# Compact RMS roots and paired projections in a two-layer diffusion backbone

## What is computed

```python
def _rmsnorm(x, w):
    xf = x.astype(jnp.float32)
    y = xf * lax.rsqrt(jnp.mean(xf * xf, axis=-1, keepdims=True) + NORM_EPS)
    return (y * w.astype(jnp.float32)).astype(x.dtype)
...
        h = _modulate(_rmsnorm(x, norm1_w[i]), sh1, sc1)
...
        o = o * lax.rsqrt(jnp.mean(o * o, axis=-1, keepdims=True) + NORM_EPS)
        return (jax.nn.silu(g) * o).reshape(b, l, hv).astype(dtype) @ w_out
...
    return _rmsnorm(x, final_norm_w)
```

## Time and profile before

| | |
|---|---|
| device time, median of 3 | 2215.78 us (2214.82 to 2217.1) |
| span of the profiled execution | 2214.5 us |
| that execution's own time | not given beside the span |
| TensorE matmul / weight load busy | 2022.2 us (91%) / 1728.0 us (78%) |
| VectorE busy | 1377.0 us (62%) |
| ScalarE busy | 764.3 us (35%) |
| GpSimd busy | 95.5 us (4%) |
| mean granted TensorE clock | 0.965 |
| chain that ended last | PE 75%, DVE 11%, issue 7%, ACT 4%, DMA 3% |

### The profile page before, as it was taken

One profiled execution on the slowest core, in us unless ns is written; L12 is line 12 of the kernel. 1 busy time (PEld: TensorE's weight loads), 2 busy tenths in 40 slices (PEclk: granted clock), 3 DMA queues, 4 the chain that ended last, 5 costly groups with the idle time before them and its releaser, 6 DMA issues.

```text
span 2214.5 us, 30605 instructions
## 1 busy us (share of the span) xinstructions
PE 2022.2 (91%) x10688; PEld 1728.0 (78%) x10688; DVE 1377.0 (62%) x2236; ACT 764.3 (35%) x1277; POOL 95.5 (4%) x161
## 2 busy tenths in 40 slices
PE   5899999999999869999999997889989779999996
PEld 5778878888887758888888886777777658788784
DVE  5665565564663677766664657667667467557376
ACT  3424223223323334312221333455545334323232
POOL 0000000000000000000000001210101000000000
PEclk9999999999999989999999998999999789999998
DMA  6230230230230112233224213211110122222222
GB/s 263 77 105 29 99 102 24 92 105 20 96 105 29 48 48 98 91 123 124 95 95 161 76 66 130 82 43 53 34 43 33 59 74 95 94 95 95 85 95 85
DMA packets 50748, 186.38 MB, mean 84 GB/s; under 512 B 5552, under 2 KB 5552, under 8 KB 50544
## 3 DMA queue, kind: packets, MB, share of 16 engines
q1 hardware_dynamic: 37248, 136.73, 17.9%
q0 software_dynamic: 13424, 48.63, 6.6%
HBM read 181.15 MB, written 4.19 MB: 84 GB/s over the span
## 4 chain that ended last, share of the span: by engine, by line
PE 75%; DVE 11%; issue 7%; ACT 4%; DMA 3%; DVEq 0%; SPq 0%; ACTq 0%; POOLq 0%
PE acc L370 60%; PE o_ps L452 4%; PE acc L561 4%; PE o_ps L540 3%; DMA ada_raw<-in_ada_dram 2%; PE acc L441 2%; PE acc L530 1%; DVE pt_lo L1369 1%; DVE h_lo L1099 1%; DMA x<-in_x_in_dram 1%; DVE ss L1027 1%; DVE nk_lo L1379 1%; DVE scratch L1090 1%; DVE w_lo L995 1%; ACT w_hi L669 1%
## 5 line engine op out<-in xcount | busy, mean ns | idle before, releaser
L370 PE MATMUL acc<-h_hi,w_hi 128*128 128x512 f32 (+1 forms) x1824 | 521.5, 351 | 41.5 <-DVE h_lo L1099 35.6
L370 PE MATMUL acc<-h_lo,w_hi 128*128 128x512 f32 (+1 forms) x1824 | 515.9, 348 | 0.0
L370 PE MATMUL acc<-h_hi,w_lo 128*128 128x512 f32 (+1 forms) x1824 | 515.6, 348 | 0.0
L669 ACT ACTIVATE w_hi<-raw 128x1024 fp32r<-128x1024 f32 x232 | 244.9, 1056 | 598.7 <-PE acc L370 598.5
L995 DVE TENSOR_TENSOR w_lo<-raw,w_hi 128x1024 fp32r<-128x1024 f32 x232 | 283.7, 1223 | 253.9 <-ACT w_hi L669 248.0
L370 PEld LDWEIGHTS acc<-h_hi,w_hi 128*128 128x128 f32 x1824 | 292.8, 189 | 96.4 <-issue 37.2
L370 PEld LDWEIGHTS acc<-h_hi,w_lo 128*128 128x128 f32 x1824 | 292.8, 189 | 45.5
L370 PEld LDWEIGHTS acc<-h_lo,w_hi 128*128 128x128 f32 x1824 | 292.9, 189 | 44.9
L370 PE MATMUL acc<-act_hi,w_hi 128*128 128x512 f32 (+1 forms) x528 | 163.0, 363 | 14.5 <-DVE act_lo L1273 12.2
L1113 DVE SCALAR_TENSOR_TENSOR x<-acc,mod,x 128x512 f32 (+3 forms) x136 | 81.9, 637 | 143.6 <-PE acc L370 138.6
L370 PE MATMUL acc<-act_lo,w_hi 128*128 128x512 f32 (+1 forms) x528 | 162.3, 361 | 0.0
(11 more groups left out here) (182 smaller groups left out, 2987.2 us busy)
## 6 DMA issues: line engine op xcount, KB each, us to landing
raw<-in_weights_dram SPq DMA_DIRECT2D x232, 512.0 KB, 3.3
ada_raw<-in_ada_dram POOLq DMA_DIRECT2D x80, 512.0 KB, 3.6
ada_start<-in_ada_first_dram SPq DMA_DIRECT2D x4, 2048.0 KB, 21.8
x<-in_x_in_dram SPq DMA_DIRECT2D x1, 3072.0 KB, 23.3
park_dram<-x POOLq DMA_DIRECT2D x1, 2048.0 KB, 8.1
rel<-in_bias_dram POOLq DMA_DIRECT2D x16, 128.0 KB, 2.4
x<-park_dram POOLq DMA_DIRECT2D x1, 2048.0 KB, 8.9
out_dram<-x SPq DMA_DIRECT2D x8, 256.0 KB, 2.0
```

The source lines that it names most:

```text
L370: mm = nc.tensor.matmul(tile[:, c0:c0 + cn], wt[:, b * P:(b + 1) * P], mv[:, n, c0:c0 + cn], start=(n == 0 and m == 0), stop=(n == last an ...
L669: nc.scalar.activation(w_hi[i][:, :], raw[i][:, :], ACT.Copy).then_inc(hi_split, 1)
```

## The change

`ss` is turned into token sums the other way round: each 128 x 128 piece of `ss` is the stationary operand and two columns of ones the moving one, so that the sums of 128 tokens come out one per partition; six such matmuls leave 128 x 6 sums (`token_sums`). ScalarE takes the root of 128 x 6 (after a root of one column that is issued before the wait), VectorE inverts 128 x 6 and multiplies the identity by it, which fills `ss` with six diagonal blocks. A matmul of ones by these blocks (`spread_roots`) leaves the inverse roots, the same in every partition, in the first two banks of `o_ps`; VectorE reads them from there. The sums lie in the fourth bank.

The two projections behind each norm become `project_two`: both weight chunks and both PSUM tiles are taken at once, and for each k all matmuls of both projections are issued, so that both end together. In layer 1 the values and keys then use the two tiles `acc[1]` and `acc[0]`. In the heads, the token sums follow gate chunk 1, the spread stands inside the projection of gate chunk 2 before its fourth k, the root and the inverse come before gate 1's Silu and its split. At the end one operation takes the place of two per chunk. (Left out below: declarations, `open_at` moved up, `take_keys` with the tile as an argument, the same edit of tallies.)

```diff
@@ -213,6 +214,8 @@
         o_ps = ctx.enter_context(nc.psum_tensor("o_ps", [P, VC, LAT], F32))
+        sums = o_ps[:, 3, 0:2 * TT]
+        spread = o_ps[:, 0:2, :].rearrange("p a t -> p (a t)")
         side = [o_ps[:, 2 * i:2 * i + 2, :].rearrange("p a t -> p (a t)") for i in range(2)]
...
@@ -382,7 +392,7 @@
                         pe.wait_ge(set_up, 1)
-                        ones_tile(KC, PARTS)
+                        token_sums(KC, TOK)
                     pe.wait_ge(ada_start_in[i], 16)
...
@@ -390,27 +400,54 @@
                 mm.then_inc(ada_started, 1)
-            def ones_tile(n, parts, on_side=False):
+                spread_roots(PARTS)
+            def token_sums(n, width):
                 pe.wait_ge(sq_added, squares_added.up(n))
-                tile = open_side(B.next_at(0)) if on_side else open_acc()
+                for t in range(width // P):
+                    mm = nc.tensor.matmul(sums[:, 2 * t:2 * t + 2], ss[:, t * P:(t + 1) * P], ones[:, 0:2], start=True, stop=True)
+                mm.then_inc(sums_done, 1)
+            def spread_roots(parts):
+                pe.wait_ge(diag_done, diags.up())
                 for c0, cn, _ in parts:
-                    mm = nc.tensor.matmul(tile[:, c0:c0 + cn], ones[:, :], ss[:, c0:c0 + cn], start=True, stop=True)
-                mm.then_inc(side_full if on_side else acc_full, 1)
+                    mm = nc.tensor.matmul(spread[:, c0:c0 + cn], ones[:, :], ss[:, c0:c0 + cn], start=True, stop=True)
+                mm.then_inc(spread_done, 1)
+            def project_two(parts, ready, tiles=None):
+                jobs = []
+                for j in range(2):
+                    w = next_chunk()
+                    jobs.append((open_acc() if tiles is None else open_at(tiles[j]), w))
+                for n in range(KC):
+                    ready(n)
+                    for tile, w in jobs:
+                        for m, (wt, mv) in enumerate(((w[0], h_hi), (w[0], h_lo), (w[1], h_hi))):
+                            for c0, cn, _ in parts:
+                                mm = nc.tensor.matmul(tile[:, c0:c0 + cn], wt[:, n * P:(n + 1) * P], mv[:, n, c0:c0 + cn],
+                                                      start=(n == 0 and m == 0), stop=(n == KC - 1 and m == 2))
+                        if n == KC - 1:
+                            mm.then_inc(acc_full, 1)
             def h_ready(first):
...
             def head_front(hd, first):
-                ready = None
                 if first:
                     ready = h_ready(h_split.now())
                     h_split.up(KC)
-                project(h_hi, h_lo, PARTS, ready)
-                value_tiles[0] = opened[0]
-                project(h_hi, h_lo, PARTS)
-                value_tiles[1] = opened[0]
+                    project_two(PARTS, ready)
+                    for n, i in enumerate((A.turn, 1 - A.turn)):
+                        value_tiles[n] = (i, A.taken[i].now())
+                else:
+                    project(h_hi, h_lo, PARTS)
+                    value_tiles[0] = opened[0]
+                    project(h_hi, h_lo, PARTS)
+                    value_tiles[1] = opened[0]
                 if not first:
...
@@ -474,8 +511,8 @@
                 project(h_hi, h_lo, PARTS)
-                ones_tile(VC, PARTS, on_side=True)
-                project(h_hi, h_lo, PARTS)
+                token_sums(VC, TOK)
+                project(h_hi, h_lo, PARTS, lambda n: spread_roots(PARTS) if n == 3 else None)
                 project(h_hi, h_lo, PARTS)
...
@@ -498,8 +535,9 @@
                     if first:
                         h_split.up(KC)
-                    with turns(pe, size, A.steps(2) + [(chunk, 2)]):
-                        project(h_hi, h_lo, parts, ready if first else None)
+                        project_two(parts, ready)
+                    with turns(pe, size - first, A.steps(2) + [(chunk, 2)]):
+                        project(h_hi, h_lo, parts)
                         project(h_hi, h_lo, parts)
...
@@ -623,17 +655,17 @@
             head_attention()
-            steps = [(chunk, 16), (squares_added, VC), (p_split, 8), (o_left, 2), (gates_split, VC)]
-            with turns(pe, RH - 1, A.steps(HEAD_TILES + 8) + B.steps(HEAD_SIDE, 1) + steps):
+            steps = [(chunk, 16), (diags, 1), (squares_added, VC), (p_split, 8), (o_left, 2), (gates_split, VC)]
+            with turns(pe, RH - 1, A.steps(HEAD_TILES + 8) + B.steps(HEAD_SIDE) + steps):
                 head_front(None, False)
...
             out_projection()
-            ones_tile(KC, PARTS)
+            token_sums(KC, TOK)
+            spread_roots(PARTS)
             ffn(PARTS)
-            ones_tile(KC, PARTS)
-            ready = h_ready(h_split.now())
-            part(values_or_keys(), 0, KC, ready)
-            part(values_or_keys(), 0, KC)
+            token_sums(KC, TOK)
+            spread_roots(PARTS)
+            project_two(PARTS, h_ready(h_split.now()), (1, 0))
             part(queries(), 0, KC)
...
@@ -648,15 +680,18 @@
                     project(no_hi, no_lo, LATENT)
-            ones_tile(KC, LATENT)
+            token_sums(KC, LAT)
+            spread_roots(LATENT)
             ffn(LATENT)
-            ones_tile(KC, LATENT)
+            token_sums(KC, LAT)
+            spread_roots(LATENT)
         @block.scalar
...
             raws, slot = [Tally(), Tally()], [0]
+            roots = Tally()
             squares_added, normed, dists, ropes, p_split, value_steps, o_left = (Tally() for _ in range(7))
...
@@ -691,10 +726,12 @@
                 squares_added.up(n)
-            def root(n, width, on_side=False):
-                i, tile = wait_side(B.next_at(0)) if on_side else wait_full()
-                nc.scalar.activation(ss[:, 0:width], tile[:, 0:width], ACT.Sqrt, bias=EPS, scale=1.0 / n)\
-                  .then_inc((side_taken if on_side else acc_taken)[i], 1)
+            def root(n, width):
+                nc.scalar.activation(nothing[:, :], ones[:, 0:1], ACT.Sqrt)
+                act.wait_ge(sums_done, roots.up())
+                t = width // P
+                nc.scalar.activation(rms[:, 0:t], sums[:, 0:2 * t].rearrange("p (t c) -> p t c", c=2)[:, :, 0],
+                                     ACT.Sqrt, bias=EPS, scale=1.0 / n).then_inc(root_done, 1)
             def x_final():
...
@@ -792,8 +829,8 @@
                 squares(vo, VC, TOK)
+                root(RV, TOK)
                 gate(1, *wait_full())
-                root(RV, TOK, on_side=True)
                 def gated_hi(g):
...
@@ -861,7 +899,7 @@
             steps += [(value_steps, 7), (o_left, 2), (gated_chunks, 4), (gates_split, 4)]
-            with turns(act, RH - 1, A.steps(HEAD_TILES + 8) + B.steps(HEAD_SIDE, 1) + steps):
+            with turns(act, RH - 1, A.steps(HEAD_TILES + 8) + B.steps(HEAD_SIDE) + [(roots, 1)] + steps):
                 head_front(False)
...
@@ -1020,11 +1059,18 @@
                 nc.vector.tensor_tensor(ss[:, 0:width], ss[:, 0:width], S[j][:, 0:width], ALU.add).then_inc(sq_added, 1)
-            def one_over(width, on_side=False):
-                i, _, _, after = B.next_at(0) if on_side else A.next()
-                dve.wait_ge((side_taken if on_side else acc_taken)[i], after)
-                step(nc.vector.reciprocal(ss[:, 0:width], ss[:, 0:width]))
+            def one_over(width):
+                t = width // P
+                dve.wait_ge(root_done, roots.up())
+                step(nc.vector.reciprocal(rms[:, 0:t], rms[:, 0:t]))
+                nc.vector.tensor_tensor(ss[:, 0:width].rearrange("p (t q) -> p t q", q=P),
+                                        ident.rearrange("p (t q) -> p t q", t=1).to_broadcast([P, t, P]),
+                                        rms[:, 0:t].rearrange("p (t q) -> p t q", q=1).to_broadcast([P, t, P]),
+                                        ALU.mult).then_inc(diag_done, 1)
+            def rooted():
+                dve.wait_ge(spread_done, roots.now())
             def take_start():
...
@@ -1079,11 +1125,12 @@
                     one_over(width)
+                rooted()
                 def scaled(k):
                     for c0, cn, c in parts:
-                        o, a, b = (z[:, c0:c0 + cn] for z in (S[2 + k % 2], x[:, k, :], ss))
+                        o, a, b = (z[:, c0:c0 + cn] for z in (S[2 + k % 2], x[:, k, :], spread))
                         if by_column and c == 0:
...
@@ -1209,7 +1256,7 @@
                 def gated(g):
-                    step(nc.vector.tensor_tensor(vo[:, g, :], vo[:, g, :], ss[:, :], ALU.mult))
+                    step(nc.vector.tensor_tensor(vo[:, g, :], vo[:, g, :], spread[:, 0:TOK], ALU.mult))
                     nc.vector.tensor_tensor(vo[:, g, :], vo[:, g, :], S[2 + g % 2][:, 0:TOK], ALU.mult).then_inc(gate_mul, 1)
...
@@ -1217,8 +1264,9 @@
                                             vg_hi[:, g * TOK:(g + 1) * TOK].bitcast(F32), ALU.subtract).then_inc(gate_lo, 1)
+                one_over(TOK)
```

(10 more changed lines are left out.)

28 lines of the change are left out of this document (16 added, 12 removed).

## The result

The changed kernel takes 2195.84 us (median of 4 runs, 2193.89 to 2197.65) against 2216.44 for the kernel before in the same series (4 runs, 2214.82 to 2221.16): a ratio of 0.9904, with a 95% interval of 0.9887 to 0.9921. A second series gave 2193.09 against 2213.80, ratio 0.9903 (0.9888 to 0.9919). The forecast was 2200.3 with a range of 2193 to 2210: the direction and the range hold, and the gain is 5 us larger than forecast. The profiled spans are 2195.8 and 2214.5, so 18.7 us have to be found in the trace where the forecast had 15.5.

The account below looks back on a forecast made before the run. TensorE's waits for `h_lo` behind norms were taken as the bound: a serial chain and a projection fed at VectorE's pace. Terms sum to -15.5 from span 2214.5: 2199.0, plus offset 1.3, gives 2200.3 us, range 2193 to 2210.

Parts of the forecast that it names:

- head 0: First head: its chain of waits starts when the first value projection is taken, now at the pair's end: +3.3 us.
- FFN of layer 1: Pair behind norm 2 of layer 1, 512 columns: 16.05 us with the weight split behind it, against 15.95: 0.
- FFN of layer 0: Pair behind norm 2 of layer 0: ends 18.4 us after the first `h_lo`, then split and wait, against 24.1: -3.0 us.
- The norm's chain: Sums to first scaled product: -3.0 us at norm 2 of layer 0, -3.0 and -2.1 at norms 1 and 2 of layer 1.
- Rival (d): Diagonal product in every chain slower than 0.96 us: gain gone at 3.6, 2226 us at 4.95; chance 0.05.
- Token sums in the heads: In four heads the sums are extra work on a TensorE without a gap: 4 x 1.28 = +5.1 us.
- rival (b): Token sums in the heads do not speed up with the clock: 4 x 1.28 us more, 2205.4 us; chance 0.08.
- Now that is E: Head 0: the first value projection is taken only at the pair's end E, 19.3 us after first `h_lo`, not 16.06.
- But both weight slots are held until E: Behind a pair: the next weight chunk is split only after the pair's end E, TensorE waiting 2.45 us with handovers.
- Values, keys, queries: Layer 1, first `h_lo` to first scores: 30.3 us against 37.4, 7 less, of which -6.3 was taken.
- rival (a): TensorE falls to the low clock level in waits of 2.45 to 3.35 us behind pairs: +6.5, 2207 us; chance 0.17.
- Rival (c): What TensorE saves in the pairs is waited for behind them: the -3.0 and -6.3 vanish, 2209.6 us; chance 0.10.

Follow-up runs that it names:

- the kernel with old roots: Changed kernel, in the heads alone with the full ones tile, root and reciprocal of the kernel before: 2189.12 us, ratio 0.9888 to the kernel before.
- the pairs alone: Kernel before with `project_two` alone, its old roots kept: 2203.53 us against 2213.56, ratio 0.9958.
- fillers: Changed kernel with old head roots, head 0's value projections one after the other, plus filler matmuls in TensorE's waits at four norms: 2178.02 us, ratio 0.9836.
- The early spread: Changed kernel with each head's spread ahead of the first k block of the next projection, not the fourth: 2210.24 us against 2215.25 before, ratio 0.9981.

## Why the prediction was right, and where its sizes were off

The direction and the mechanism of each part came out as said. That the sum came as near as 3.2 us of the profiled span is partly luck: head 0 and the FFN of layer 1 came out 1.9 and 4.2 us below their terms, the rest of the heads and the FFN of layer 0 1.5 and 1.3 above, and these partly cancel.

- **The norm's chain** (-3.0, -3.0, -2.1): measured -3.0, -3.1, -2.2. Its prices came from the nearest rows: root 0.18 (said 0.2), inverse 0.19 (0.2), diagonal 0.96 (0.96), sums 2.41 and 1.05 (2.2 and 1.1), spread 2.93 and 2.07 (2.9 and 1.9). Rival (d), the diagonal, is out by its own row. The sizes of single chains move with the clock: norm 2 of layer 0 takes 9.7 to 10.9 us to the first k block in the traces with compact roots and the dummy, where 10.6 is the changed kernel's first profile and 13.6 the kernel before.
- **Token sums in the heads** (+5.1): a record takes half of 0.213 at the high level, 12 in 1.25 us (190.75 to 192.00; 1.28 was said). So the choice of the half over the full price was right, and the row refutes rival (b). The Trainium skill (TensorE: Matmul & The Clock Gate, LDWEIGHTS) gives a load of 128 columns as 128 / 1.2 ns, 0.107 us, so an estimate by its figure is 1.28 for the twelve loads at either level, and not the 2.56 that the prediction took for it. The trace agrees with that at the high level (1.25) and not at the low one (2.41 to 2.72): the loads followed the clock. The other 1.6 us of the heads' +6.6 have no shown cause. The slower out projections (0.2, 0.6 and 0.6 us in the first three) come near it, but the kernel with old roots has them at no cost in sum; in the second profile the stretch from the first k block to norm 2 grew by 6.2 us in place of 8.0.
- **Head 0** (+3.3): measured +1.4 in the profile, 1.3 to 2.2 over the pairs of kernels. The step that failed is "Now that is E": the pair ends at 18.96 (19.3 was said), but the first value tile is full one k block of one projection before its end, at 17.9, and 17.9 - 16.06 = 1.9. That E came near is in part two errors against each other: no row shows its 5.9 us at the low level, the pair's records are at the low pitch for 4.0 us (59.22 to 63.18); and a block took 1.06, not 1.04. In the second profile head 0 with its sums is 0.9 longer than before, less than the 1.25 of its sums, so the size of this term is uncertain by over 1 us.
- **FFN of layer 0** (-3.0): the same step, "But both weight slots are held until E". The first slot is free one block earlier, so the split that was priced at 2.45 behind E overlaps the last block and leaves a wait of 1.51. The point at which the next chunk starts is 3.9 earlier than before (20.25 against 24.18 after the first k block), where 3.0 was said, and with the pairs alone the group ends 3.8 earlier. In the changed kernel's first profile the loop behind it gives 2.3 back (118.81 against 116.48 for the same projections, 1.06 against 1.04 a block at full clock), which makes -1.7; in its second the next chunk starts at 21.10, that loop is at 116.59 and the whole group at 137.69 against 140.66, -3.0. In the ten traces of the pair without fillers this group takes 136.6 to 140.1 us, so the term is known to 2 us at best.
- **Values, keys, queries** (-6.3): -5.8. The wait for the queries' chunk was 2.12, where 3.35 was said, again one block less; but behind it the clock fell for some 3.4 us. That is rival (a), at one of the three places where a pair leaves a wait, and one of the signs of being wrong that the prediction names; behind the waits of 1.51 and 1.90 it did not fall in any of the eleven traces with a pair. Behind the queries' wait (2.12 to 2.14 in all eleven) it fell in six, and the way to the first scores is 31.5 to 31.8 us; in the other five it did not, and it is 30.0, 7.4 less than before and near the 7 of the forecast's own sum. So the -6.3 lies between two outcomes. (Windows ahead of and behind 1403.4, then behind the same wait in the kernel with old roots in the heads:)

```profile
1401.30:1403.40 2.10, 0.04 (x1) 0.04 (x1) 1.23 (x1) 2.08 (x3) 0.00 (x0) 1.00 1.00 295
1403.40:1409.00 5.60, 5.60 (x18) 4.49 (x19) 5.33 (x5) 2.77 (x4) 4.16 (x6) 0.70 0.41 143
...
1398.90:1404.50 5.60, 5.58 (x25) 4.57 (x26) 5.28 (x5) 2.83 (x4) 4.06 (x6) 1.00 0.40 149
```

- **FFN of layer 1** (0): -4.2, the largest miss. The pair itself gave -0.4 as the sum had it. Of the rest, 1.5 is pitch in the first two down projections, which goes with 32 bytes of address, 1.5 one fall of the clock that did not happen, and 0.8 is in the third group. The term that failed is the 0 for all that the change does not touch.
- **Start** (-2.3): -1.95; the sums began at 36.29 in this profile, when the ones matmul of before began at 35.80, as `x` landed later. **End** (-4.2): -4.3; the products run at 5.36/8 = 0.67 each against 1.12 for two.
- **Rival (c)**, the pair brings nothing: refuted by the pair alone, 0.9958.
- Rival (d)'s price for a late diagonal in the heads, 4(d - 2.4), counted the wait alone. The early spread shows 3.7 us per head for a wait of 1.5, so that branch would have cost over twice as much. Its other part, 4(d - 0.96), is said to cover the four norms and the start, which are five places; it prices four.
